# Reordering the attention stage of a decoder step: where the queries' broadcast, the samples' probabilities and values, the normalising and the output weights stand in each engine's program

## The reference, cut to what matters

```
qkv = h @ w_qkv                                  # 264 rows: 256 prompt tokens, 8 samples
s   = (q . k) / 8 - slope[head] * (t - s)        # causal for the prompt
p   = softmax(s)
out = (p @ v) @ w_o                              # v of the prompt, or cached pages and the own v
```

## Time and profile before

| | |
|---|---|
| median of 3 runs | 1955.16 us (1954.64 to 1956.35) |
| the profiled execution | 1954.54 us |
| its span in the profile | 1952.4 us, 2.1 us under its time |
| mean granted TensorE clock of it | 0.964 |
| busy: PE, DVE, ACT, POOL | 93%, 77%, 62%, 1% of the span |

### The profile page before, as it was taken

How to read it: one execution, slowest core, us unless ns; L and a number is a source line. 1 busy time by engine, 2 the same in 40 slices (tenths; PEclk the granted TensorE clock), 3 DMA queues, 4 the chain that set the end, 5 groups by cost and what they waited for, 6 DMA issues and landing times.

```text
span 1952.4 us, 26550 instructions
## 1 busy us (share of the span) xinstructions
PE 1819.3 (93%) x9702; PEld 1447.8 (74%) x9702; DVE 1504.1 (77%) x1568; ACT 1201.4 (62%) x1115; POOL 18.2 (1%) x73
## 2 busy tenths in 40 slices
PE   6999799999899789999999999999999999999997
PEld 3777479999887766776767677676777787787775
DVE  3686455555798589898998989899788787887884
ACT  2243244444457268787888878788666677676673
POOL 2000000000000000000000000000000000000000
PEclk8899799999899879999999999999999999999998
DMA  9676776655725259999999999999999798998970
GB/s 329 236 260 236 257 265 213 223 169 181 248 87 185 77 216 376 381 392 397 378 387 387 380 386 391 397 376 387 359 336 366 286 359 316 333 354 315 333 289 22
DMA packets 221526, 579.22 MB, mean 297 GB/s; under 512 B 10478, under 2 KB 73398, under 8 KB 221437
## 3 DMA queue, kind: packets, MB, share of 16 engines
q1 hardware_dynamic: 220429, 573.98, 80.2%
q0 software_dynamic: 1024, 4.25, 0.7%
HBM read 574.79 MB, written 4.35 MB: 297 GB/s over the span
## 4 chain that ended last, share of the span: by engine, by line
PE 60%; DVE 16%; issue 7%; ACT 5%; DVEq 1%; DMA 0%; ACTq 0%; SPq 0%; PEldq 0%
PE banks L980 18%; DVE w_lo L1937 12%; PE banks L968 12%; PE banks L492 11%; PE banks L938 4%; ACT w_hi L1297 4%; PE banks L791 3%; PE banks L811 2%; PE banks L924 1%; PE banks L884 1%; PE banks L902 1%; PE banks L571 1%; PE banks L948 1%; PE banks L551 1%; PE banks L597 1%
## 5 line engine op out<-in xcount | busy, mean ns | idle before, releaser
L1937 DVE TENSOR_TENSOR w_lo<-ring,w_hi 128x2048 fp32r<-128x2048 f32 x420 | 947.3, 2289 | 155.3 <-ACT w_hi L1297 155.2
L1297 ACT CAST w_hi<-ring 128x2048 fp32r<-128x2048 f32 x420 | 798.3, 1911 | 276.8 <-PE banks L980 177.5
L980 PE MATMUL banks<-w_hi,x_s 128*128 128x512 f32 x672 | 281.0, 418 | 41.7 <-DVE w_lo L1937 37.2
L980 PE MATMUL banks<-w_hi,x_m 128*128 128x512 f32 x896 | 288.6, 398 | 2.2 <-DVE w_lo L1937 2.2
L968 PE MATMUL banks<-w_hi,g_buf 128*128 128x512 f32 x784 | 285.4, 405 | 4.6 <-DVE w_lo L1937 2.6
L980 PE MATMUL banks<-w_lo,x_s 128*128 128x512 f32 x672 | 267.0, 397 | 0.0
L968 PE MATMUL banks<-w_lo,g_buf 128*128 128x512 f32 x560 | 221.4, 395 | 0.0
L1450 DVE TENSOR_TENSOR w_lo<-ring,w_hi 128x1024 fp32r<-128x1024 f32 x124 | 143.9, 1204 | 91.8 <-ACT w_hi L1106 90.1
L980 PEld LDWEIGHTS banks<-w_hi,x_s 128*128 128x128 f32 x672 | 127.1, 189 | 111.9 <-DVE w_lo L1937 82.7
L1106 ACT CAST w_hi<-ring 128x1024 fp32r<-128x1024 f32 x124 | 121.4, 1032 | 127.8 <-PE banks L492 46.0
L980 PEld LDWEIGHTS banks<-w_hi,x_m 128*128 128x128 f32 x896 | 168.3, 188 | 42.8 <-DVE w_lo L1937 2.6
(11 more groups left out here) (377 smaller groups left out, 2045.3 us busy)
## 6 DMA issues: line engine op xcount, KB each, us to landing
ring<-in_moe_w_dram SPq DMA_DIRECT2D x420, 1024.0 KB, 6.5
ring<-in_ada_w_dram SPq DMA_DIRECT2D x48, 1024.0 KB, 5.9
ring<-in_ffn_w_dram SPq DMA_DIRECT2D x30, 1024.0 KB, 7.4
ring<-in_attn_w_qkv_dram SPq DMA_DIRECT2D x12, 1024.0 KB, 10.8
ring<-in_conv_w_pw_dram SPq DMA_DIRECT2D x12, 1024.0 KB, 12.0
ring<-in_cache_k_dram SPq DMA_DIRECT2D x16, 512.0 KB, 4.9
ring<-in_cache_v_dram SPq DMA_DIRECT2D x16, 512.0 KB, 5.0
ring<-in_attn_w_o_dram SPq DMA_DIRECT2D x4, 1024.0 KB, 10.4
```

Source lines behind the costliest of these rows:

```text
L980: mm = pe.matmul(bk[:, b, :], x, y, start=(k == 0 and i == 0), stop=(k == KC - 1 and i == len(x_passes(k, hi, lo)) - 1), skip_group_check= ...
L1297: act.copy(w_unit(n)[0], ring[:, pos_of(n), :]).then_inc(ev("moe_hi_ready"), 1)
L1937: dve.tensor_tensor(lo, ring[:, pos_of(n), :], hi.bitcast(F32), ALU.subtract).then_inc(ev("moe_lo_ready"), 1)
```

## The change

- TensorE broadcasts the queries of a step's pages after the scores of the step, no more ahead of its half 0. VectorE's `sample_scores` moves with it: from between `normalise` and the first half to behind the scores and the split.
- The multiplying of the probabilities goes from VectorE to ScalarE, as four activations with a scale for each pair; VectorE keeps the reciprocals. TensorE counts two announcements for each head. ScalarE does it at the start of step n, ahead of its copy of half 0.
- ScalarE also copies the conditioning rows (`ada_row`), in place of VectorE.
- In step 7 TensorE transposes the samples' probabilities and spreads the own one before the scores of pair 7; VectorE makes the samples' probabilities ahead of its wait for half 1.
- In the tail the even samples' values come first, then pairs 6 and 7, then the odd samples' values, each half followed by the own values' product.
- `wo` block 0 is loaded after all value pages. The two splits of `wo` blocks 0 and 1 on ScalarE and VectorE go behind pair 7.

The diff, without its parts on names of loop variables:

```diff
-        wo_block(0)
         for n in (*range(0, NS, 2), *range(1, NS, 2)):
             pages(("V", n), cache_v[0], n, "pe")
-        for j in range(1, 4):
+        for j in range(4):
             wo_block(j)
...
@@ TensorE
-                    pe.wait_ge(ev("probs_ready"), 2 * c + hh + 1)
+                    pe.wait_ge(ev("probs_ready"), 2 * (2 * c + hh + 1))
...
                 blk = ("qkv", KV[n])
-                for i in PAGES_AT[n]:
-                    q_all(i)
...
                 dense([blk], h_hi, h_lo, between)
                 if n >= 1:
                     scores(n - 1)
+                for i in PAGES_AT[n]:
+                    q_all(i)
                 if n in ROWS_AT:
                     filler()
                 if n == KC - 1:
+                    pe.wait_ge(ev("sample_probs_ready"), 1)
+                    bk = group("probsT_s")
...
+                    bk = group("PD")
+                    filled(pe.matmul(bk[0:NS, 0:P], e8[:, :], diag[:, :], start=True, stop=True))
                     scores(KC - 1)
...
             ada_turn()
             turn("v_s", lambda c: hT[:, c, TP:T], NS, 2)
-            pe.wait_ge(ev("sample_probs_ready"), 1)
-            bk = group("probsT_s")
...
-            attend_turn(KC - 2)
-            attend_values(KC - 2)
-            pe.wait_ge(ev("sample_probsT_ready"), 1)
...
+            def sample_values(e):
...
+                    if e:
+                        mm = pe.matmul(pv[half], PD[:, :], v_s[:, half * 512:(half + 1) * 512], start=False, stop=True, skip_group_check=True)
                         mm.then_inc(ev("values_used"), 1)
+                if e == 0:
+                    mm.then_inc(ev("even_values_used"), 1)
...
+            pe.wait_ge(ev("sample_probsT_ready"), 1)
+            sample_values(0)
+            attend_turn(KC - 2)
+            attend_values(KC - 2)
+            attend_turn(KC - 1)
+            attend_values(KC - 1)
+            pe.wait_ge(ev("v_ready"), 1)
+            sample_values(1)
...
@@ ScalarE
+            def normalise(c):
+                for hh in range(2):
+                    act.wait_ge(ev("sums_ready"), 2 * c + hh + 1)
+                    for i, cols in enumerate((slice(0, P), slice(P, 384))):
+                        k = 12 + 2 * hh + i
+                        act.activation(P_p[:, hh, cols], P_p[:, hh, cols], ACT.Copy, scale=st_p[:, k:k + 1]).then_inc(ev("probs_ready"), 1)
...
+                if n >= 2:
+                    normalise(n - 2)
                 keep_block(0)
...
                 if n >= 1:
                     exps(n - 1)
+                if n in ROWS_AT:
+                    ada_row(*fillers[n - 1])
                 if n == KC - 1:
-                    split_behind(("qkv", KV[KC - 2]))
+                    normalise(KC - 2)
...
             exps(KC - 1)
             keep_attention(KC - 2)
+            normalise(KC - 1)
             attend(KC - 1)
             keep_attention(KC - 1)
+            split_behind(("qkv", KV[KC - 2]))
             split_behind(("qkv", KV[KC - 1]))
...
@@ VectorE, normalise
                     step(dve.reciprocal(st_p[:, 12 + 2 * hh:14 + 2 * hh], st_p[:, 8 + 2 * hh:10 + 2 * hh]))
-                    settle()
-                    for i, cols in enumerate((slice(0, P), slice(P, 384))):
-                        k = 12 + 2 * hh + i
-                        step(dve.tensor_scalar(P_p[:, hh, cols], P_p[:, hh, cols], st_p[:, k:k + 1], None, ALU.mult))
-                    announce("probs_ready")
+                    announce("sums_ready")
...
@@ VectorE, the loop
                 if n >= 2:
                     normalise(n - 2)
-                for i in PAGES_AT[n]:
-                    sample_scores(i)
...
                 if n >= 2:
                     attend_turn(n - 2)
+                if n == KC - 1:
+                    sample_probs()
                 kept((blk, 1))
                 if n >= 2:
                     attend_values(n - 2)
                 if n >= 1:
                     scores(n - 1)
-                if n < KC - 2:
-                    split_behind(blk)
+                    if n < KC - 2:
+                        split_behind(blk)
+                for i in PAGES_AT[n]:
+                    sample_scores(i)
+                    if i == 0:
+                        split_behind(blk)
...
                 if n in ROWS_AT:
-                    filler()
+                    ada_row_kept(*fillers[n - 1])
+                    if len(pending) > 1:
+                        ada_turn()
                 if n == KC - 1:
-                    sample_probs()
-                    dve.wait_ge(ev("exps_ready"), 4 * (KC - 2) + 4)
+                    bk = take("probsT_s")
...
+                    announce("sample_probsT_ready")
+                    normalise(KC - 2)
                     scores(KC - 1)
-                    split_behind(("qkv", KV[KC - 2]))
...
@@ VectorE, the tail
-            normalise(KC - 2)
             ada_turn()
             sample_rows("v_s", v_s)
-            bk = take("probsT_s")
...
             attend_values(KC - 1)
+            split_behind(("qkv", KV[KC - 2]))
             for half in range(2):
                 dve.wait_ge(ev("values_used"), half + 1)
```

More of the change, by code:

```diff
@@ L707, in _ @@
                 if n == KC - 1:
+                    pe.wait_ge(ev("sample_probs_ready"), 1)
+                    bk = group("probsT_s")
+                    for i in range(PAGES):
+                        mm = pe.transpose(bk[:, i * P:(i + 1) * P], P_s[:, i * P:(i + 1) * P], ident[:, :])
+                    filled(mm)
+                    bk = group("PD")
+                    filled(pe.matmul(bk[0:NS, 0:P], e8[:, :], diag[:, :], start=True, stop=True))
                     scores(KC - 1)
@@ L722, in _ @@
             turn("v_s", lambda c: hT[:, c, TP:T], NS, 2)
-            pe.wait_ge(ev("sample_probs_ready"), 1)
-            bk = group("probsT_s")
[L725 to L729, removed]
-            attend_turn(KC - 2)
-            attend_values(KC - 2)
-            pe.wait_ge(ev("sample_probsT_ready"), 1)
             pv = [stat, stat2]
-            for half in range(2):
-                pe.matmul(pv[half], PD[:, :], v_s[:, half * 512:(half + 1) * 512], start=True, stop=False, skip_group_check=True)
-            for e in range(2):
+            def sample_values(e):
                 for n in range(e, NS, 2):
@@ L745, in _ @@
                             mm = pe.matmul(pv[half][32 * q:32 * q + 32, :], PT_s[:, g, q, e, :], V[:, g, half * 512:(half + 1) * 512],
[L746 to L749, removed]
+                                           start=(e == 0 and g == 0), stop=False, skip_group_check=True)
+                    if e:
+                        mm = pe.matmul(pv[half], PD[:, :], v_s[:, half * 512:(half + 1) * 512], start=False, stop=True, skip_group_check=True)
                         mm.then_inc(ev("values_used"), 1)
+                if e == 0:
+                    mm.then_inc(ev("even_values_used"), 1)
                 for n in range(e, NS, 2):
[L752 to L755, removed]
+                    used[index[("V", n)]] = (ev("values_used"), 2) if e else (ev("even_values_used"), 1)
+            pe.wait_ge(ev("sample_probsT_ready"), 1)
[6 more added lines that the diff above has]
+            sample_values(1)
             pe.wait_ge(ev("own_pv_ready"), 1)
@@ L1731, in _ @@
                     normalise(n - 2)
-                for i in PAGES_AT[n]:
-                    sample_scores(i)
-                    if i == NS - 1:
-                        dve.sem_inc(ev("sample_scores_ready"), 1)
                 kept((blk, 0))
@@ L1745, in _ @@
                     scores(n - 1)
-                if n < KC - 2:
-                    split_behind(blk)
+                    if n < KC - 2:
[4 more added lines that the diff above has]
+                        split_behind(blk)
+                    if i == NS - 1:
+                        dve.sem_inc(ev("sample_scores_ready"), 1)
                 if n in ROWS_AT:
-                    filler()
+                    ada_row_kept(*fillers[n - 1])
+                    if len(pending) > 1:
+                        ada_turn()
                 if n == KC - 1:
-                    sample_probs()
-                    dve.wait_ge(ev("exps_ready"), 4 * (KC - 2) + 4)
+                    bk = take("probsT_s")
+                    for e in range(2):
+                        ins = dve.tensor_copy(PT_s[:, :, :, e, e * H:(e + 1) * H],
+                                              bk[:, 0:PAST].rearrange("p (g q e h) -> p g q e h", g=PAGES, q=4, e=2)[:, :, :, e, :])
+                        (drained if e else step)(ins)
+                    bk = take("PD")
+                    drained(dve.tensor_copy(PD, bk[0:NS, 0:P]))
+                    announce("sample_probsT_ready")
+                    normalise(KC - 2)
                     scores(KC - 1)
-                    split_behind(("qkv", KV[KC - 2]))
                 kept(("v_tok" if is_v else "k_tok", g))
```

(9 more changed lines are left out.)

## The result

The changed kernel takes 1965.35 us (median of 5 runs, 1964.31 to 1971.31; two of them took 1971), the kernel before 1955.16 on the same chip. The ratio is 1.0061, with an interval of 1.0042 to 1.0079: slower. The profiled execution took 1965.35 us with a span of 1963.6.

A forecast was written before the change was run, and what follows sets the result against it. TensorE and VectorE were taken to run abreast in the steps, the tail as a chain through all engines. Terms 18.5 - 1.9 + 0 - 7.2 = +9.4 us on 1954.5 gave 1963.9, median 1964.5; range 1955 to 1971.5.

The forecast's parts named there:

- Steps 3 to 6: Attention steps 3 to 6: sample scores ahead of the reciprocals make TensorE wait; 77.2 us, 18.5 more than 58.7, bounds +14.5 to +22.5.
- The chain: In steps 3 to 6: scores, split, sample scores, reciprocals at M + 12.8, ScalarE's scaling, transposes, half 1 at M + 15.2.
- M: The end of half 1 of an attention step, from which the forecast counts times in us.
- The rival in which the clock drops each step: Steps 3 to 6: every half 1 takes 5.1 us; in all +15.2, 1970.3 us; chance 0.17.
- the one in which it stays up: Steps 3 to 6: every half 1 takes 3.1 us at the full clock; in all +0.7, 1955.9 us; chance 0.17.
- Steps 0 to 2: First attention steps: TensorE no longer waits for the queries' rows before half 0; 1.9 us less, bounds 2.8 and 0.8.
- Step 7: Last attention step, which has no sample scores: no change; bounds 2.0 us less to 0.7 more.
- The tail: From step 7's end to the output projection: even samples' product starts earlier; 32.1 us against 39.3, 7.2 less, bounds 9 to 2.4.
- the rival of loads beside GpSimd's stores: Tail: last value page and `wo` block 0 load twice as long, tail 37 us; in all +14.2, 1969.3 us; chance 0.06.
- The sum: Whole kernel: 18.5 - 1.9 + 0 - 7.2 = 9.4 us more than the profiled execution's 1954.5; median 1964.5 us.
- The faster rival: Steps 3 to 6: sample scores done before half 0 ends, 13.7 us a step; in all -13.0, 1942.1 us; chance 0.10.
- The multiplying on ScalarE: Steps 3 to 6: gives VectorE back 1.1 us a step, worth nothing, and puts 1.6 on the chain in its place.

The follow-up runs named there:

- the runs with the stores held back: GpSimd's stores of new keys and values put behind the tail: in the changed kernel 1967.08 us; in that with pages a step later and loads reordered 1939.8 us.
- the ten profiles named above: Profiles of kernels with the stores in their old place; from output projection to end they take between 1718.9 and 1723.4 us.
- the kernel with the scores back: Changed kernel with the queries' broadcast and sample scores back ahead of half 0, the rest of the change kept: 1941.4 us, ratio 0.9924.
- The two kernels with the loads reordered: Scores ahead of half 0, each page a step later, key pages behind their step's other loads: 1937.8 us; the same with the stores behind the tail: 1939.8 us.

## Why the prediction was right

The forecast was 1964.5 us and slower with a chance of 0.72; measured were 1965.35 and slower. By its terms, in the profiled execution:

**Steps 3 to 6: forecast +18.5, measured +20.35** (79.05 - 58.7), within the bounds. The chain was right to a few tenths: reciprocals at M + 12.8 forecast and 12.7 measured; TensorE's wait 3.9 and 3.94; half 1 from M + 15.2, measured 15.0. The size that was off is half 1: I had taken 4.1, the middle between the two clocks, and it took 5.3, 5.3, 3.8 and 4.6, on the mean 4.75. Each of the four steps shows a clock under 1.00, in two of them through nearly all of half 1 and in two through a part of it. The rival in which the clock drops each step was thus half true, and the one in which it stays up was not. The Trainium skill (TensorE: Matmul & The Clock Gate, HAM oscillation — how this bites in real kernels) says that a wait which recurs in a loop drops the clock in each turn; the trace agrees, with mean clocks of 0.83, 0.83, 0.91 and 0.91 in the four steps and a wait of 3.9 to 4.0 in each. The Trainium skill has the next turn start at the lower clock there; that all of half 1 would run at it was the prediction's own reading, and its 5.1 was nearer to the 4.75 than my middle of 4.1.

**Steps 0 to 2: forecast -1.9, measured -0.15**, outside the bounds (0.8 to 2.8 less). Step 2 ends at 114.05, 114.20 before. The stage itself began 0.7 later in this execution. The first reciprocal was forecast for 105.9 and came at 106.62, so that part of the working stands; half 1 of step 2 then ran 5.1 at the lower clock, the upper bound. What is beyond the bound is the later start.

**Step 7: forecast 0, measured -0.75**, within its bounds.

**The tail: forecast -7.2, measured -6.9** (32.4 against 39.3), but by two errors that cancel. The even product ran at the full clock (3.64, not 5.0), the odd one only in its second half (3.44, then 1.92 for as many matmuls); pairs 6 and 7 took 8.6, not 9.2. So the last value product was done at M + 25.9 (237.09 - 211.15), not M + 28.4. Then came 6.5 us to the projection where I had 3.75: the step that failed is that `wo` block 0 is in time. I had its cast at M + 19.6; it came at M + 23.6. That is the rival of loads beside GpSimd's stores, to which I gave 0.06. It held in its mechanism, as the runs with the stores held back show: without the stores those 6.5 us are 3.7, what I had. It cost some 2.7 us (32.4 - 29.65), not the 4.8 that I had priced; the same tail with the stores took 30.9 to 34.4 in six other profiles, and 29.65 and 29.05 in the two without. The Trainium skill (DMA: Bandwidth & Descriptors, Issuing engines are not separate DMA queues) says that transfers issued by different engines run on the same transfer engines; the traces agree, with 14.2 us for a load beside the stores and 8.4 without.

**The sum** is +12.55 at the output projection, where I had +9.4. It is +11.2 at the end of the span and 10.2 in the medians; the later stages, which the change leaves alone, were 1.35 us shorter, less than the 4.5 by which they differ among the ten profiles named above. So the median within 0.9 us of the forecast is in part luck: by the terms of the sum the forecast was 3.15 short, 1.85 of it in steps 3 to 6 and 1.75 in steps 0 to 2, and the later stages and the choice of the profiled executions gave 2.35 of that back.

**The faster rival**, that VectorE's order does not bind, had its point of decision at VectorE's time from M to the reciprocals, under some 8.5 us. With 12.7, as here, the step is 19 to 20. The point does not decide alone: with 7.1 the step is 16 to 18, since the banks hold next; with the scores behind the reciprocals and ahead of half 0 it is 13.55. That last kernel came out at a ratio of 0.9924, near the one that the rival had named (1942.1 of 1955.16 is 0.9933), but by another order and other terms: its step 2 ends 1.05 later than before (115.25, 114.20), where the rival had 1.9 less.

**The multiplying on ScalarE**: that what VectorE gets back by giving it away is worth nothing holds in the changed order, by the 2.3 and 2.35 from reciprocals to half 1. In the old order, of which the prediction says nothing, it was not shown to be worth anything by itself either (0.9985, 0.9971 to 1.0000).

## What to carry to other kernels

When work is moved in one engine's program, list what now stands behind it and who waits for that: here 5 us of work that nobody waits for before step 7 was put ahead of 0.5 us of reciprocals that all of the next step waited for, and it cost 20 us in four steps. A good change can hide behind a bad one, so undo one part at a time: with that single move undone, the kernel is 0.76% faster than before (ratio 0.9924) and no longer 0.61% slower, and with each page a step later and its loads in the order of use 0.95% (0.9905). Before moving work earlier, look at what limits it next (the bank sixth behind, the ring slot, the load beside a store); in these runs each hold that was taken away showed the next one.

## What was not expected of the hardware

TensorE can run at the lower clock without a gap in its rows. With the multiplying alone on ScalarE, step 4 is busy for all of its time and still has a mean clock of 0.80; the same step of the kernel with the scores back, with one row fewer in the trace, runs at 1.00. Windows of step 4 of the one, then of the other:

```profile
131.00:147.70 16.70, 16.70 (x105) 12.63 (x104) 11.39 (x19) 7.81 (x20) 0.00 (x0) 0.80 0.82 282
```

```profile
128.80:142.35 13.55, 13.55 (x104) 9.92 (x103) 10.69 (x18) 8.26 (x21) 0.00 (x0) 1.00 0.88 310
```

What stands ahead of half 0 there are small matmuls: conditioning rows from 32 columns of weights, transposes, broadcasts from 8 rows. Whether half 0 behind them starts at the lower clock differs from one execution to the next, by up to 3 us in a step. The two kernels with the loads reordered have the same program up to the stores; step 3 is 13.90 at a clock of 1.00 in the profile of the one (above), and in the profile of the other, with the stores held back, without a wait either:

```profile
107.50:124.20 16.70, 16.70 (x105) 12.52 (x104) 11.29 (x19) 8.30 (x21) 0.00 (x0) 0.80 0.78 266
```

A few such steps would cover the spread of one kernel's times (the one with the loads reordered took 1932.4 to 1941.8). That they do is not shown, since there is one profile of each kernel, and what decides the clock there was not tried.
